# Taking the filler products on TensorE out of a two-layer decoder trunk, all but the forty at its start

## The reference, cut to what matters

```
h = x
for i in range(2):
    xn = rms_norm(h, norm_mix[i])
    h = h + (diff_attention(xn, ...) if i == 0 else pool_mixer(xn, ...))
    xn = rms_norm(h, norm_ffn[i])
    h = h + (swiglu(xn, ...) if i == 0 else moe_swiglu(xn, ...))   # top 2 of 8 experts
    gate = sigmoid(rms_norm(h, norm_ple[i]) @ ple_w_gate[i])
    h = h + gate * (p[i] @ ple_w_proj[i])
```

## Time and profile before

| what | value |
|---|---|
| median of 3 runs | 1403.01 us (1402.98 to 1404.18) |
| profiled execution | 1404.94 us |
| its span, first to last instruction | 1403.2 us |
| mean granted TensorE clock | 0.999 of full speed |
| TensorE busy | 1376.4 us, 98% of the span |
| VectorE / ScalarE / GpSimd busy | 83% / 68% / 5% |
| data moved | 421.41 MB, 300 GB/s over the span |

### The profile page before, as it was taken

One profiled execution on the slowest core, in us unless ns is written; L12 is line 12 of the kernel. 1 busy time (PEld: TensorE's weight loads), 2 busy tenths in 40 slices (PEclk: granted clock), 3 DMA queues, 4 the chain that ended last, 5 costly groups with the idle time before them and its releaser, 6 DMA issues.

```text
span 1403.2 us, 17313 instructions
## 1 busy us (share of the span) xinstructions
PE 1376.4 (98%) x6700; PEld 1143.0 (81%) x6700; DVE 1163.7 (83%) x956; ACT 955.5 (68%) x870; POOL 68.1 (5%) x96
## 2 busy tenths in 40 slices
PE   8998999999999999999999999999999999999998
PEld 7876888888887888888888888888888888888877
DVE  6786665557799889889988988998898898889876
ACT  5666544446677777777777677777777777776765
POOL 2110800000200000000000000000000000000000
PEclk9999999999999999999999999999999999999999
DMA  9732755555199989999999999999999999999970
GB/s 309 254 121 56 247 204 184 184 198 166 54 388 362 328 327 349 361 373 369 355 381 343 349 375 372 355 362 367 350 334 376 373 360 372 364 342 357 370 291 31
DMA packets 197586, 421.41 MB, mean 300 GB/s; under 512 B 13048, under 2 KB 37376, under 8 KB 197504
## 3 DMA queue, kind: packets, MB, share of 16 engines
q1 hardware_dynamic: 197504, 420.30, 82.7%
HBM read 419.22 MB, written 1.05 MB: 300 GB/s over the span
## 4 chain that ended last, share of the span: by engine, by line
PE 88%; DVE 5%; ACT 3%; issue 1%; DMA 1%; SPq 0%; POOL 0%; ACTq 0%; DVEq 0%; POOLq 0%
PE ps L316 25%; PE ps L318 24%; PE ps L317 24%; PE ps L843 5%; DVE w_lo L296 3%; PE ps L841 3%; ACT w_hi L279 2%; PE ps L823 2%; PE ps L973 1%; PE ps L992 1%; PE ps L840 1%; DMA raw<-in_attn_w_qkv_dram 1%; ACT y_hi L1412 1%; PE ps L655 0%; PE ps L682 0%
## 5 line engine op out<-in xcount | busy, mean ns | idle before, releaser
L296 DVE TENSOR_TENSOR w_lo<-raw,w_hi 128x2048 fp32r<-128x2048 f32 x383 | 876.1, 2297 | 148.9 <-ACT w_hi L279 146.2
L279 ACT ACTIVATE w_hi<-raw 128x2048 fp32r<-128x2048 f32 x384 | 734.1, 1915 | 138.8 <-PE ps L318 136.3
L316 PE MATMUL ps<-w_hi,xe_hi 128*128 128x512 f32 x560 | 222.1, 397 | 2.8 <-DVE w_lo L296 2.8
L318 PE MATMUL ps<-w_hi,xe_lo 128*128 128x512 f32 x560 | 218.4, 390 | 0.0
L317 PE MATMUL ps<-w_lo,xe_hi 128*128 128x512 f32 x560 | 218.1, 389 | 0.0
L316 PE MATMUL ps<-w_hi,h_t_hi 128*128 128x512 f32 x536 | 210.4, 393 | 1.8 <-DVE h_t_lo L1790 1.8
L318 PE MATMUL ps<-w_hi,h_t_lo 128*128 128x512 f32 x536 | 209.5, 391 | 0.0
L317 PE MATMUL ps<-w_lo,h_t_hi 128*128 128x512 f32 x536 | 209.2, 390 | 0.0
L316 PE MATMUL ps<-w_hi,xb_hi 128*128 128x512 f32 x336 | 133.2, 396 | 0.8 <-DVE w_lo L296 0.8
L318 PE MATMUL ps<-w_hi,xb_lo 128*128 128x512 f32 x336 | 131.1, 390 | 0.0
L317 PE MATMUL ps<-w_lo,xb_hi 128*128 128x512 f32 x336 | 130.8, 389 | 0.0
(11 more groups left out here) (275 smaller groups left out, 1526.2 us busy)
## 6 DMA issues: line engine op xcount, KB each, us to landing
raw<-in_moe_w_gate_dram SPq DMA_DIRECT2D x112, 1024.0 KB, 6.9
raw<-in_moe_w_up_dram SPq DMA_DIRECT2D x111, 1024.0 KB, 6.5
raw<-in_moe_w_down_dram SPq DMA_DIRECT2D x111, 1024.0 KB, 6.7
raw<-in_attn_w_qkv_dram SPq DMA_DIRECT2D x11, 1024.0 KB, 12.5
raw<-in_ffn_w_gate_dram SPq DMA_DIRECT2D x11, 1024.0 KB, 5.2
raw<-in_ffn_w_up_dram SPq DMA_DIRECT2D x11, 1024.0 KB, 5.2
raw<-in_ffn_w_down_dram SPq DMA_DIRECT2D x11, 1024.0 KB, 4.9
raw<-in_ple_w_gate_dram SPq DMA_DIRECT2D x8, 1024.0 KB, 7.0
```

Source lines behind the costliest of these rows:

```text
L279: nc.scalar.activation(w_hi[:, u % SPLIT, :], raw_slot(u), ACT.Copy).then_inc(hi_ready, 1)
L296: nc.vector.tensor_tensor(w_lo[:, u % SPLIT, :], raw_slot(u), w_hi[:, u % SPLIT, :].bitcast(F32), ALU.subtract).then_inc(lo_ready, 1)
L316: nc.tensor.matmul(out, x[0], w[0], start=first, stop=False)
L318: return nc.tensor.matmul(out, x[1], w[0], start=False, stop=last)
```

## The change

All calls of `keep_clock` but the one at the start are removed, and with them the parameter and the table that only they used. The waits and all other instructions keep their order. 172 of 212 filler products go: 60 + 12 around the norm, 60 ahead of the pooling mixer, 24 + 16 in the router.

```
-        FREE_BANK = {1: 0, 4: 3}
...
-            def transpose_norm(n, quarters=range(4), warm=True, turns=0):
+            def transpose_norm(n, quarters=range(4), turns=0):
...
                     last.then_inc(xs_transposed, 1)
-                    if n in FREE_BANK and warm:
-                        keep_clock(FREE_BANK[n], 6)
...
-                    transpose_norm(1, (0, 1), warm=False)
+                    transpose_norm(1, (0, 1))
...
-            keep_clock(0, 60)
             transpose_norm(1, (2, 3))
...
             pe.wait_ge(sig_ready, 3)
-            keep_clock(4, 60)
             pe.wait_ge(bands_ready, 1)
...
-            transpose_norm(4, warm=False)
+            transpose_norm(4)
...
             last.then_inc(logits_ready, 1)
-            keep_clock(7, 24)
 
             pe.wait_ge(mask_ready, 1)
...
             nc.tensor.matmul(ps[:, 1, 16:24], ones16[:, :], mask[:, 1, :], start=False, stop=True).then_inc(counted, 1)
-            keep_clock(7, 16)
```

## The result

The changed kernel takes 1410.7 us in the median of five runs (1409.75 to 1412.25); the kernel before took 1403.52 us in its five (1402.98 to 1404.18). The ratio is 1.005 with a 95% interval of 1.0039 to 1.0062: slower, as forecast, but by 7.2 us and not by 4.6, and beyond the range, which ended at 1410.0. The profiled execution took 1412.25 us with a span of 1410.5 us, 7.3 us more than the one before.

A forecast was written before the change was run, and what follows sets the result against it. TensorE's stream was taken to bound the kernel. Clock falls at norm, pooling mixer and router (1.7 + 1.6 + 1.3 - 0.05, say 4.6 us) on the median of 1403.01 gave 1407.6 us, range 1404.8 to 1410.0.

The forecast's parts named there:

- The bound: TensorE, busy for 98% of the span; any delay of its stream before the dense stage and experts delays the end equally.
- the late spell: Half-rate clock in the earlier trace, 1362.3 to about 1365.7 us, behind a 1.78 us wait of TensorE; priced at 1.6 us.
- The fillers cost nothing: At all three places removing the fillers gains between nothing and 0.15 us; 0.05 taken, from an earlier gather in the router.
- The quiet stretches: TensorE left idle 4.3 us at the norm, 4.6 at the pooling mixer, 0.46, 2.0 and 0.9 in the router; all bring falls.
- Rivals 1 and 4: 1: router's stretch brings no fall, 1406.3 us, chance 0.12; 4: clock holds in all three stretches, 1402.9 us, chance 0.05.
- The norm: Four turns at half rate start the dense stage 0.4 us later, which then runs slow; 1.7 us, bounds 0.8 and 2.0.
- The pooling mixer: Split products right behind the gap run at half rate; 1.6 us, as the late spell cost, bounds 0.7 and 3.0.
- the opening: The kernel's start, almost 6 us at half rate in the earlier trace; coming out of idleness there cost 3.0 us.
- The router: The gather's first 16 products at half rate delay VectorE's copy behind them; 1.3 us, bounds 0 and 1.8.
- The sum: Norm 1.7, pooling mixer 1.6 and router 1.3, less 0.05 gained: 4.55, say 4.6 us slower.
- Rival 2: Long half-rate spells, as at the opening, at all three places: 6.8 us slower, 1409.8 us; chance 0.10.
- rival 3: The late spell goes away: 3.0 us slower, 1406.0 us, chance 0.12; or another short gap falls: 1409.2 us, chance 0.04.

The follow-up runs named there:

- e9_router24: Only the router's 24 fillers ahead of the wait for the mask taken out of the kernel before; median 1405.11 us, ratio 1.0004 (0.9995 to 1.0013).
- e6_half_front: The kernel before with the pooling mixer's 60 fillers cut to 30 at the front of the gap; median 1406.38 us, ratio 1.0014.
- e5_wide: The kernel before without the pooling mixer's 60 fillers, nine 512-column products behind the gap instead; median 1408.32 us, ratio 1.0032.
- e3_router: Only the router's 40 fillers taken out of the kernel before; median 1405.65 us, ratio 1.0011 (1.0002 to 1.0020).
- e2_pool: Only the 60 fillers ahead of the pooling mixer taken out of the kernel before; median 1407.16 us, ratio 1.0024 (1.0015 to 1.0033).
- e11_sixes: Only the two groups of six fillers behind the norm's quarters 2 and 3 taken out of the kernel before; median 1405.27 us, ratio 1.0004.
- e7_half_mid: The kernel before with 30 fillers in the middle of the pooling mixer's gap instead of 60; median 1404.48 us, ratio 1.0006.

## Why the prediction was wrong

- **The bound: right.** (One reading was too strong: the slices of the earlier trace rows don't show full speed throughout but 0.9 or more, and the late spell lies in one of them.) TensorE's stream sets the end. In both profiles of the changed kernel, every delay at the three places is found again unchanged at the next stage, and the sum of the stages gives the span within 0.1 us.
- **The fillers cost nothing: right**, and the 0.05 us that I had them cost in the router isn't there either: the gather came 1.16 us behind the count in both.
- **The quiet stretches: right** in length (4.24, 4.61, 2.03 and 0.88 us measured), and all three brought the clock down in every profile of a kernel without the fillers of that place. Rivals 1 and 4 are out.
- **The norm, 1.7 us: too small.** The first 0.4 us, the turns at half rate, came out at 0.43. The dense stage lost 2.0 us (1.9 in the second profile) where I had 1.3; in all 2.4, beyond my upper bound of 2.0; alone 2.3 in the median and 3.0 in the profile.
- **The pooling mixer, 1.6 us: this is the step that failed.** "I take 1.6, the row's own price" assumed that what the late spell cost, 3.4 us at half rate, is what a fall costs. The spell here was 6.8 us in both profiles of the changed kernel and 10.2 when alone, nearly all of it on working time: 3.0 and 3.9 us, 3.5 in the median. The upper bound of 3.0, read off the opening, was itself too low. What failed is the length and not the price of a short spell: in two profiles (e9_router24, with all 60 fillers in place, and e6_half_front) the mixer met a spell of 3.4 us, and from its first product to the sixteen turns it took 12.30 and 12.29 us, 1.5 more than before. In e9_router24:

```profile
362.61 0.36 PE L890 MATMUL ps<-xe_hi,a_all 128*128 128x256 f32 x1 [1.24 <-DVE a_all L1864]
...
374.91 1.91 PE L562 MATMUL ps<-ident,resid 128*128 128x128 f32 x16
```

- **The router, 1.3 us:** 0.9 in both profiles of the changed kernel, 1.7 in the profile with this place alone and 2.0 us in its median. Inside the bounds or just beyond, and not what put the sum too low.
- **The sum.** 2.4 + 3.0 + 0.9 = 6.3 us against 4.6. Rival 2, long spells everywhere (6.8 us, 1409.8), was the nearest case, and I gave it 0.10. What lifts the median from there to 6.7 to 7.2 us wasn't followed stage by stage. The profiled execution of the first five had a mean granted clock of 0.992, and two others, 1410.7 and 1410.76 us, had 0.991 and 0.990, some 3 and 6 us more of low time: longer or further spells are the likely reason, and such as the single removals show (10.2 us at norm and mixer, 6.8 at the router).
- **The late spell.** It was absent in both profiles after, as rival 3 had it, and present in two of the fourteen profiles in all; in medians it plays no part, so the 1.6 us that rival 3 took off the median forecast were not there to be taken.
- **The pages of the Trainium skill.** "TensorE: Matmul & The Clock Gate" (Terms) charges half of the throttled time. With the low time now measured, 6.8 + 6.8 + 3.4 = 17.0 us in the second profile, that is 8.5 us; the stages lost 6.3, above all because part of the norm's spell lay on waits (2.4 of 3.4 us) and part of the gather's on products behind those that the path needs (0.9 of 1.7). The measurement decides, and the direction in which I had corrected the rule holds. Its advice against long idle gaps between bursts (in "Why this matters for your kernels") was right here, though falls also came behind idle pieces of 0.9 to 2.9 us. The page also says, in Part 1, that the ramp differs from run to run because the observation runs freely; the trace agrees, with the attention spell in some executions of identical code and spells of 6.8 and 10.2 us at one place.

What stays open: why a spell at the mixer lasts 6.8 or 10.2 us and at 1362 us 3.4. The kind of work behind the gap (e5_wide) is a candidate that one profile favours. How long the idle stretch was is another: at the norm and the mixer the spells of 6.8 us and more came behind more than 4 us of idleness or behind the narrow fillers, and those of 3.4 us behind pieces of 0.9 to 2.9 us. But the router's pieces of 2.03 and 0.88 us were followed by 6.8 us in e3_router and by 3.4 in both profiles of the changed kernel, and the slower executions of e6_half_front, with 8 to 11 us of low time behind 2.92 us of idleness, point to long spells there too. So the length alone doesn't settle it.

## What to carry to other kernels

When a bound engine's clock depends on its recent work, price the removal of its fillers by the delay of everything behind them at the lower clock and by the longest spell seen, not by the shortest: one fall at these three places cost 0.9 to 3.9 us, up to two and a half times what the single row showed. Fillers that stood in idle time were free here. Those of 128 columns held the clock where those of 8 did not; a gap filled to 1.24 us of its end was followed by a fall in one of seven profiles; with 2.32 or 2.92 us left idle in one piece there was a fall in both profiles. Whether fillers between short pieces of thin work are needed too is open. Don't take one profile for the typical execution: compare its time and clock with those of the other runs. Look for the fall in windows of 20 us or less: 40 slices of a long span hide it.

## What the runs showed of the hardware that was not expected

- The clock stayed at 0.50 for 3.4, 6.8 or 10.2 us, and for no length between (falls behind the last product, cut off by the end, left aside), and in e2_pool it did so although TensorE worked without a break for 9.4 us.
- Idle pieces each below 0.9 us (0.87 and 0.84), with eight small turns between, were followed by a fall in the profile of e11_sixes. In the profile of e9_router24 it fell at the mixer with all 60 fillers in place, the only one of seven such profiles, so they don't exclude a fall.
- The same gap may bring a fall or not: that of 2.16 us in attention did in six of fourteen profiles, that of 1.78 us near 1361 us in two of thirteen.
- 116 products of 8 columns in 3.06 us did not hold it.
- A fall can come while fillers already run again (e7_half_mid, at 361 us) or 1.9 us into the real work (e6_half_front, at 364.7 us).
